# Taking the last eight tokens out of the expert-output matmuls of a 320-token sweep and adding them on VectorE

## What is computed

```
a = jax.nn.gelu(jnp.einsum('ted,td->te', u[ib], xb), approximate=False)
return jnp.einsum('te,ted->td', gb * a, v[ib])
```

## Time and profile before

| | |
|---|---|
| median of 3 runs | 4030.26 us (4028.16 to 4032.87) |
| the profiled execution's own time | 4045.91 us |
| its span | 4043.8 us |
| TensorE busy | 3878.7 us, 96% |
| table v, first to last matmul | 3099.6 to 4013.5 us |

### The profile page before, as it was taken

One profiled execution on the slowest core, in us unless ns is written; L12 is line 12 of the kernel. 1 busy time (PEld: TensorE's weight loads), 2 busy tenths in 40 slices (PEclk: granted clock), 3 DMA queues, 4 the chain that ended last, 5 costly groups with the idle time before them and its releaser, 6 DMA issues. The chain is left out here.

```text
span 4043.8 us, 70070 instructions
## 1 busy us (share of the span) xinstructions
PE 3878.7 (96%) x26200; PEld 3702.3 (92%) x26200; DVE 3054.3 (76%) x4083; ACT 1422.9 (35%) x2046; POOL 1570.5 (39%) x1349
## 2 busy tenths in 40 slices
PE   7999999999999887999999999999998999999997
PEld 7989988999999665989899999999997999999997
DVE  6875167777777433878589999999976888888887
ACT  5884122222223222223333333333333333333332
POOL 0000022233233112234116566666776455555551
PEclk9999999999999898999799999999998999999998
DMA  7988888999999796889579899888999999999996
GB/s 272 341 307 298 290 292 327 355 375 364 370 372 367 285 380 261 297 323 356 211 267 326 321 331 325 318 313 299 340 347 315 360 348 346 342 345 346 342 345 240
DMA packets 336051, 1310.12 MB, mean 324 GB/s; under 512 B 48912, under 2 KB 105392, under 8 KB 266304
## 3 DMA queue, kind: packets, MB, share of 16 engines
q1 hardware_dynamic: 201680, 646.09, 43.7%
q0 software_dynamic: 108848, 629.71, 42.2%
q10 hardware_dynamic: 25344, 31.99, 2.1%
HBM read 1237.86 MB, written 69.77 MB: 323 GB/s over the span
## 5 line engine op out<-in xcount | busy, mean ns | idle before, releaser
L2365 POOL DMA_INDIRECT routes_scratch<-gate_sums,route x384 | 463.8, 1208 | 165.8 <-issue 104.2
L130 PE MATMUL acc<-x_hi,w_hi 128*128 128x448 f32 x1296 | 476.9, 368 | 11.2 <-DVE w_lo L119 6.5
L130 PE MATMUL acc<-x_lo,w_hi 128*128 128x448 f32 x1296 | 474.9, 366 | 0.0
L130 PE MATMUL acc<-x_hi,w_lo 128*128 128x448 f32 x1296 | 474.8, 366 | 0.0
L114 ACT ACTIVATE w_hi<-w_raw 128x1024 fp32r<-128x1024 f32 x242 | 256.3, 1061 | 605.2 <-DMA w_raw<-in_w_gate 263.0
L119 DVE TENSOR_TENSOR w_lo<-w_raw,w_hi 128x1024 fp32r<-128x1024 f32 x242 | 295.3, 1222 | 178.7 <-ACT w_hi L114 178.0
L2777 POOL TENSOR_TENSOR tile_full<-act_and_gate 128x320 f32<-128x320 f32 x120 | 310.2, 2585 | 261.2 <-DVE tile_lo L2882 173.6
L2154 ACT ACTIVATE w_hi_a<-w_raw 128x1024 fp32r<-128x1024 f32 x270 | 279.3, 1057 | 287.4 <-PE acc L2954 250.2
L2172 PE MATMUL acc<-h_hi,w_hi_b 128*128 128x320 f32 (+1 forms) x1152 | 367.3, 319 | 13.3 <-DVE w_lo_b L2162 13.3
L2172 PE MATMUL acc<-h_hi,w_hi_a 128*128 128x320 f32 (+1 forms) x1152 | 370.4, 322 | 9.0 <-DVE w_lo_a L2162 7.7
L2172 PE MATMUL acc<-h_lo,w_hi_a 128*128 128x320 f32 (+1 forms) x1152 | 367.0, 319 | 0.0
(11 more groups left out here) (519 smaller groups left out, 10430.9 us busy)
## 6 DMA issues: line engine op xcount, KB each, us to landing
w_raw<-in_w_peer_u SPq DMA_DIRECT2D x256, 512.0 KB, 5.4
w_raw<-in_w_peer_v SPq DMA_DIRECT2D x256, 512.0 KB, 5.7
w_first<-in_w_gate SPq DMA_DIRECT2D x96, 512.0 KB, 4.9
w_raw<-in_w_gate SPq DMA_DIRECT2D x96, 512.0 KB, 7.1
w_first<-in_w_z SPq DMA_DIRECT2D x66, 512.0 KB, 5.2
w_raw<-in_w_z SPq DMA_DIRECT2D x66, 512.0 KB, 7.7
k_ring<-in_cache_k SPq DMA_DIRECT2D x64, 512.0 KB, 7.6
v_ring<-in_cache_v POOLq DMA_DIRECT2D x64, 512.0 KB, 8.6
```

The lines of the kernel that those rows point to most:

```text
L130: last = nc.tensor.matmul(dst, l_, r_[:, cc, 0:cn], start=(cc == first and p_ == 0), stop=(cc == last_c and p_ == 2))
L2365: pool.indirect_dma_start(route_dram, bass.IndirectOffsetOnAxis(ap=route[0:ROWS[b], b, n:n + 1], axis=0), gsum[0:ROWS[b], h % SUMS, b - 1, ...
```

## The change

Only 312 columns are left in the matmuls, tiles and sums of table v; the activations, routes and `out_t` are cut to them. Tokens 312 to 319 are computed as 8 tokens x 128 experts = 8 gathers of 128 rows: partition 16 t + j of gather k holds the row of rank 8 j + k of token t. SyncE sends the experts, routes and gates of the eight tokens through DRAM to turn them onto 128 partitions. GpSimd fetches the activations with eight indirect DMAs of one float for each partition, multiplies them by the gates, and issues the gathers, the first after step 3, then one in each place marked in the code. VectorE adds each gathered buffer, times its weight, into `sum8` (`last_row`), four matmuls with a 0/1 matrix add the 16 partitions of each token, and VectorE adds that to `x1`. There is one buffer for these rows.

```diff
+            def last_gather(k):
+                nc.gpsimd.tensor_copy(stage_8[:, 0:1], e8[...k...]).then_inc(s_8sg, 1)
+                pool.wait_ge(s_8sg, k + 1)
+                pool.sem_inc(s_8tick, 1)
+                pool.indirect_dma_start(row8[:], None, a["peer_v"], bass.IndirectOffsetOnAxis(ap=stage_8[:, 0:1], axis=0)).then_inc(s_8gat, 16)
...
-            with pool.Fori(1, (NTILE - GRP) // 2) as i:
+            rows(1, True)
+            pool.wait_ge(s_8ld, 48)
+            for k in range(VTOK):
+                pool.indirect_dma_start(a8[:, k:k + 1], None, acts_dram.rearrange("n p (t o) -> (n p t) o", o=1), bass.IndirectOffsetOnAxis(ap=r8[:, k:k + 1], axis=0)).then_inc(s_8a, 16)
+            pool.wait_ge(s_8a, 16 * VTOK)
+            nc.gpsimd.tensor_tensor(w8[:], a8[:], g8[:], ALU.mult).then_inc(s_8w, 1)
+            last_gather(0)
+            with pool.Fori(2, GRP) as i:
+                rows(i, True)
+            with pool.Fori(1, NG // 2 - 1) as gg:
+                pool.wait_ge(s_8used, gg + 1)
+                last_gather(gg)
+                with pool.Fori(0, GRP) as j:
+                    rows(GRP * gg + j, True)
+            pool.wait_ge(s_8used, VTOK)
+            last_gather(VTOK - 1)
+            with pool.Fori(GRP * (NG // 2 - 1), (NTILE - GRP) // 2) as i:
                 rows(i, True)
...
+            def last_row(k):
+                dve.wait_ge(s_8w, 1)
+                dve.wait_ge(s_8gat, 16 * k)
+                dve.wait_ge(s_8used, k)
+                nc.vector.scalar_tensor_tensor(out=sum8[:], in0=row8[:], scalar=w, in1=sum8[:], op0=ALU.mult, op1=ALU.add).then_inc(s_8used, 1)
...
+                nc.vector.memset(sum8[:], 0.0)
+                nc.vector.memset(pick[:], 0.0).then_inc(s_8used, 1)
...
             with eng.Fori(1 if start else 0, NG // 2 - 1) as gg:
+                each_group(gg)
                 for par in range(2):
...
+                if n == 0:
+                    last_row(VTOK - 1)
+                if n == 1:
+                    last_row(VTOK)
+                if n == 2:
+                    dve.wait_ge(s_8sum, 1)
+                    nc.vector.tensor_tensor(x3, tps[0:ROWS[3]].rearrange("p a c -> p (a c)"), x3, ALU.add)
...
-                        last = nc.tensor.matmul(acc[:, s, h, 0:ND], l_, r_[:, t_, :], start=(c == 0 and p_ == 0),
+                        last = nc.tensor.matmul(acc[:, s, h, 0:NV], l_, r_[:, t_, :], start=(c == 0 and p_ == 0),
...
+                if j == 2:
+                    for g in range(4):
+                        last = nc.tensor.matmul(tps[0:ROWS[3], g, :], pick[:], sum8[:, 512 * g:512 * (g + 1)], start=True, stop=True)
```

More of the change, by code:

```diff
@@ L2705, in build @@
         s_g3, s_b3 = sem("final_g_loaded"), sem("x1_block3_reloaded")
+        VTOK = 8
+        NV = ND - VTOK
         NG = NTILE // GRP
-        t_hi = at("tile_hi", [P, 2 * GRP, ND], F32R, O_R1)
-        t_lo = at("tile_lo", [P, 2 * GRP, ND], F32R, O_R1 + 2 * GRP * ND * 4)
+        NR = P // VTOK
+        t_hi = at("tile_hi", [P, 2 * GRP, NV], F32R, O_R1)
+        t_lo = at("tile_lo", [P, 2 * GRP, NV], F32R, O_R1 + 2 * GRP * ND * 4)
         ring_v = at("ring_v", [P, 2, D], F32, O_R1 + 4 * GRP * ND * 4)
-        out_t = at("out_t", [P, KC, ND], F32, O_T)
+        out_t = at("out_t", [P, KC, NV], F32, O_T)
         O_AG = O_T + KC * ND * 4
-        ag = at("act_and_gate", [P, 2, 2, ND], F32, O_AG)
-        hf = at("tile_full", [P, 2, ND], F32, O_AG + 4 * ND * 4)
+        ag = at("act_and_gate", [P, 2, 2, NV], F32, O_AG)
+        hf = at("tile_full", [P, 2, NV], F32, O_AG + 4 * ND * 4)
         stage_e = at("expert_stage", [P, 2, 8], I32, O_AG + 6 * ND * 4)
         assert O_AG + 6 * ND * 4 + 64 <= O_EARLY
+        row8 = at("rows_of_last_tokens", [P, D], F32, O_R1 + 4 * GRP * ND * 4 + 2 * D * 4)
+        sum8 = at("sum_of_last_tokens", [P, D], F32, O_R1 + 4 * GRP * ND * 4 + 3 * D * 4)
+        place = [O_T + KC * NV * 4]
+        e8, r8 = (then(x, [P, VTOK], I32) for x in ("last_experts", "last_routes"))
+        g8, a8, w8 = (then(x, [P, VTOK], F32) for x in ("last_gates", "last_acts", "last_weights"))
+        pick = then("last_token_of_row", [P, ROWS[3]], F32)
+        stage_8 = then("last_expert_stage", [P, 8], I32)
+        assert place[0] <= O_AG
+        s_8st, s_8ld, s_8a, s_8w, s_8sg, s_8tick, s_8gat, s_8used, s_8pick, s_8sum = (sem(f"last_tokens_{x}") for x in (
+            "stored", "loaded", "acts", "weights", "staged", "tick", "gathered", "used", "pick", "summed"))
         s_xback = sem("x1_last_reloaded")
@@ L2757, in table_v_sync @@
             load_tile(GRP + 1, 1)
+            last8 = slice(ROWS[3] - VTOK, ROWS[3])
+            for k, x_ in enumerate((eidx, route, gate.bitcast(I32))):
+                sp.dma_start(last8_dram[k], x_[last8, 3, :]).then_inc(s_8st, 16)
+            sp.wait_ge(s_8st, 48)
+            for k, x_ in enumerate((e8, r8, g8.bitcast(I32))):
+                sp.dma_start(x_[:], last8_dram[k].rearrange("t (j k) -> (t j) k", k=VTOK)).then_inc(s_8ld, 16)
             with sp.Fori(1, (NTILE - GRP) // 2) as i:
@@ L2798, in table_v_gpsimd @@
                 nc.gpsimd.memset(out_t[:, 4 * k:4 * k + 4, :], 0.0).then_inc(s_clr, 1)
+            def last_gather(k):
+                nc.gpsimd.tensor_copy(stage_8[:, 0:1], e8[:, k:k + 1] if isinstance(k, int) else e8[:, bass.ds(k, 1)]).then_inc(s_8sg, 1)
+                pool.wait_ge(s_8sg, k + 1)
+                pool.sem_inc(s_8tick, 1)
+                pool.indirect_dma_start(row8[:], None, a["peer_v"], bass.IndirectOffsetOnAxis(ap=stage_8[:, 0:1], axis=0)).then_inc(s_8gat, 16)
             def rows(i, build):
@@ L2812, in table_v_gpsimd, with sweep @@
                 rows(i, False)
-        def sweep(eng, before, split, after, beside, start=None):
+        def sweep(eng, before, split, after, beside, start, each_group):
             def body(first, par, j, build=True, ahead=True, between=None):
@@ L2875, in beside @@
                     nc.scalar.activation(ms2[:, 4:5], ms2[:, 4:5], ACT.Sqrt).then_inc(s_t0, 1)
-            sweep(act, before, lambda i, s: split_hi(act, i, s, q7), lambda *_: None, beside, lambda: None)
+            sweep(act, before, lambda i, s: split_hi(act, i, s, q7), lambda *_: None, beside, lambda: None, lambda gg: None)
         def table_v_vector(dve):
@@ L2931, in beside @@
                                                    op0=ALU.mult, op1=ALU.mult).then_inc(s_y0, 1)
-            sweep(dve, lambda *_: None, lambda i, s: split_lo(dve, i, s, q7), after, beside, sums_cleared)
+            sweep(dve, lambda *_: None, lambda i, s: split_lo(dve, i, s, q7), after, beside, sums_cleared, last_row)
         def table_v_tensor(pe):
@@ L2966, in table_v_tensor @@
                     half(0, 1, j, s, h)
-            with pe.Fori(1, NG // 2) as gg:
+            with pe.Fori(1, NG // 2 - 1) as gg:
                 for par in range(2):
@@ L2971, in table_v_tensor @@
                             half(gg, par, j, s, h)
+            with pe.Fori(0, GRP // 2) as j:
+                for s, h in QUARTERS:
+                    half(NG // 2 - 1, 0, j, s, h)
+            for j in range(GRP // 2):
+                if j == 2:
+                    pe.wait_ge(s_8used, VTOK + 1)
+                    pe.wait_ge(s_8pick, 1)
+                    pe.wait_ge(s_q0, 1)
+                    for g in range(4):
+                        last = nc.tensor.matmul(tps[0:ROWS[3], g, :], pick[:], sum8[:, 512 * g:512 * (g + 1)], start=True, stop=True)
+                    last.then_inc(s_8sum, 1)
+                for s, h in QUARTERS:
+                    half(NG // 2 - 1, 1, j, s, h)
         with nc.Block() as block:
@@ L3002, in build @@
         g_fin = g_row
+        NEW = [0, P, P, ROWS[3] - VTOK]
         y = at("y", [P, 2, D], F32, O_R1)
@@ L3031, in _ @@
                         for c in range(4):
-                            last = nc.tensor.transpose(tps[0:ROWS[b], g, c * P:(c + 1) * P],
-                                                       out_t[:, 4 * g + c, COLS[b]:COLS[b] + ROWS[b]], ident[:])
+                            last = nc.tensor.transpose(tps[0:NEW[b], g, c * P:(c + 1) * P],
+                                                       out_t[:, 4 * g + c, COLS[b]:COLS[b] + NEW[b]], ident[:])
                         last.then_inc(s_ft, 1)
@@ L3048, in add @@
                 def add(b):
-                    r = ROWS[b]
+                    r = NEW[b]
                     dve.wait_ge({1: s_back[0], 2: s_back[1], 3: s_b3}[b], 16)
```

18 lines of the change are left out of this document (12 added, 6 removed).

## The result

| | before | after |
|---|---|---|
| median | 4029.31 us (4028.16 to 4032.87, 4 runs) | 4075.33 us (4057.53 to 4084.01, 4 runs) |
| ratio | | 1.0093, 95% interval 1.0068 to 1.0119 |
| the profiled execution's own time | 4045.91 us | 4057.53 us |
| table v, first to last matmul | 913.9 us | 949.7 us |

The kernel is slower, by some 0.9%. The two medians of four runs alone would give 1.0114, which lies inside the interval. The median lies 5 us above the range that was given; by the ratio the time is 4067 us, inside it. The forecast of 4046 had the sign and the place right and less than half of the size.

A forecast was written before the change was run, and what follows sets the result against it. TensorE, busy for 96% of the span, was taken to pace the stage. Columns -21.4, seven waits +26, start +9 and four matmuls +2 make +16 us, moving the median from 4030.3 to 4046 us; 8-in-10 range 4026 to 4070.

The forecast's parts named there:

- Columns, -21.4 us: Table v's 6144 matmuls: each loses 8 columns, 3.49 ns a matmul, saving 21.4 us.
- The wait at seven places: Starts of passes 1 to 7: GpSimd waits for VectorE's `last_row`, making TensorE 3.7 us late each, 26 us in all.
- the second stall: Pass starts, half 132 in the replay of pass 4: late row gather makes TensorE 3.7 us late, first stall included.
- a first stall of 1.8 us: Pass starts, half 130 in the replay of pass 4: TensorE wants weights at 3570.0, VectorE has them at 3571.8.
- Mine of 1.8 stand between.: Stalls of 1.8 us lie between earlier idle times of 1.9 (clock dip followed) and 1.5 us (none); a dip costs 1.7.
- The landing of the gather: Row gather at a pass start lands 6.0 us after issue, the median of the earlier rows.
- The start, 9 us: First pass: GpSimd's eight small indirect DMAs delay halves 10 and 12; a stall of 7 us, 9 us in all.
- Covered work: Eighth `last_row` and 64-row addition in the last pass, SyncE's small DMAs at the start: nothing; uncovered 3 and 4 us.
- the hidden wait: Rival: the lead of ScalarE, VectorE and the halves swallows the pass-start waits; 4011 to 4020 us; chance 0.12.
- the quick landing: Rival: gathers land in 5.4 to 4.8 us, a pass start costs 3.1 to 2.5; 4034 to 4041 us; chance 0.16.
- the clock case: Rival: TensorE's stalls are followed by 1.2 GHz stretches, seven dips costing 12 us; 4056 to 4075 us; chance 0.15.
- DMA as the bound: Rival: added traffic finds no room, gain void and each of 8 gathers costs 3 us; 4065 us; chance 0.07.

The follow-up runs named there:

- narrow_only: Changed kernel with everything added for the last eight tokens taken out, leaving the 312 columns; ratio to the kernel before 0.9950.
- late_gather: Changed kernel with the wait and the last tokens' gather behind the first four steps of each pass; ratio to the kernel before 1.0000.
- wait_early_gather_late: Changed kernel with GpSimd's wait still at each pass start but the last tokens' gather issued four steps later; ratio to the kernel before 1.0081.
- changed_again: The changed kernel as it is, run again for a second profile; ratio to the kernel before 1.0102.
- late_and_spread: late_gather with the start's eight small DMAs in pairs behind steps 5, 7, 9, 11 and first gather behind step 13; ratio to before 0.9994.
- row_half_pass_early: Changed kernel with VectorE taking each last tokens' row eight steps earlier, GpSimd's queue unchanged; ratio to the kernel before 1.0023.
- all_moved: late_and_spread with VectorE's last tokens' row mid-pass and GpSimd's wait and gather behind the twelfth step; ratio to the kernel before 0.9979.

## Why the prediction was right or wrong, point by point

- **Columns, -21.4 us: right.** 21 us by the passes of narrow_only, 20 by its ratio. The pace of 320 and 448 columns gave the slope; the clock alone (20.5) would have done too.
- **The wait at seven places: right mechanism, wrong size.** That moving the wait takes the stalls away (late_gather), and that the wait without its gather keeps them (wait_early_gather_late), shows the cause. The term was 7 x 3.7 = 26 us, set by the second stall, that of the late row gather. Measured over 110.0 us (the last pass without the four matmuls) it is 5.2 + 6.1 + 6.1 + 6.1 + 5.6 + 6.2 + 6.0 = 41 us. Two steps of the replay were short, and the clock came on top:
  - *"VectorE's rest of half 130 ... is there at 3571.8", a first stall of 1.8 us.* TensorE wanted it at 3557.89 + 6.86 = 3564.75 and went on at 3568.34, 3.6 us late. The chain came about 0.6 us later than reckoned, and then the pair of rests took 3.43 us where it takes 2.35 otherwise, while GpSimd ran the product of tile 73 (3566.35) and a copy. The first of the two rests took 2.3 us at all fourteen pass starts of the two profiles of the changed kernel, the second 1.2. In the prediction GpSimd was held up by VectorE; I did not ask for the other direction. The Trainium skill, "SBUF — State Buffer", section "Who interferes with whom", says that a VectorE instruction with two SBUF inputs contends with a GpSimd instruction that reads SBUF, since its second input comes through the read interface that the two share. The rows agree that they hold each other up: VectorE lost 1.08 us against a product of 0.85. The Trainium skill adds there that the order of issue decides who is blocked. By the starts in the profile that does not come out here: VectorE's rest started 0.36 us ahead of the product and was the one that took longer. The kernel before had shown the same once, in its first pass, in VectorE's pair and GpSimd's product:

```profile
3130.16 3.30 DVE L2162 TENSOR_TENSOR w_lo_b<-w_raw,w_hi_b 128x1024 fp32r<-128x1024 f32 x2
```

```profile
3130.35 0.88 POOL L2777 TENSOR_TENSOR tile_full<-act_and_gate 128x320 f32<-128x320 f32 x1
```

  - *"it lands 6.0 us after ... 3576.0", a second stall that makes it 3.7 us in all.* In pass 4 of changed_again, without a dip, the row gather was issued 7.4 us after TensorE's first matmul of the pass (replay: 6.9), and VectorE's row started at 14.0 (replay: 12.9). Half 132 was then 4.7 us late. The 1.0 us over 3.7 comes with the row: 0.5 in the chain ahead of its issue and 0.6 in its landing, with 0.1 won behind it. The longer first stall does not add to this, as it ends before.
  - *"Mine of 1.8 stand between."* The first stall was 3.4 us idle, and in the first profile a clock dip shows behind six of the seven, in the second behind five. Four shorter stalls in wait_early_gather_late, 1.6 to 1.7 us idle, had none. With a dip a pass start costs 3.6 us for the first stall and up to 2.7 for the dip: 6.1 to 6.2 where the dip is long, and the second stall is hidden in it. So the longer first stall counts in these passes, and a dip, priced at 1.7 us, adds up to 1.4 (116.2 against 114.8). Without any dip the term would be 6 x 4.8 and 4.2 (pass 7 of changed_again, up to its middle), 33 us: of the 15 us that were missing some 7 are the late row, and the other 8 are the dips and the small gaps of pass 5 (115.6, without a dip).
- **The landing of the gather: about right.** Row 64 was issued at 3565.32 and used at 3571.98, 6.7 us against 6.0, with the queues empty before it. Over the stage the median rose from 6.0 to 8.1, though. It rose as much in late_gather (8.6), which has no such stalls, and not in narrow_only (6.0), so it goes with the added work and not with the stalls.
- **The start, 9 us: low.** The first pass lost 134.6 - (125.6 - 2.6) = 11.6 us in the first profile. But first passes scatter (narrow_only, without any of the new work, has 129.1), so no more can be said than that the stall at half 10 was there, 5.7 and 8.7 us in the two profiles of the changed kernel against the 7 of the replay, and went away in late_and_spread.
- **Four matmuls, 2 us: low.** They take 3.7. The trace has eight records for the four, of 592 ns each: the single time of the earlier trace rows was that of half a matmul. The same instructions, by line:

```profile
L3044 PE MATMUL tps<-sum_of_last_tokens,last_token_of_row x8: 592/592/643, 3994.4 to 3997.5; 128*64 128x512 f32 x8
```

- **Covered work: right but for one row.** `last_row` at step 120, the addition of 64 rows and SyncE's small DMAs show no gap of TensorE in the first profile. In changed_again there is one of 1.6 us at half 242, right behind `last_row` at step 120, where VectorE had waited 2.55 us for a row's gather just before: the picture of half 146 in row_half_pass_early. The idle time that was to cover it is not always there.
- **The sum.** The columns, the seven waits, the start and the four matmuls make, in the first profile: -20.9 + 41.3 + 11.6 + 3.7 = +35.7 us, the 35.8 of the stage. Of the rivals, the hidden wait and the quick landing are out; the clock case (4056 to 4075) was nearest, though the dips and the small gaps of pass 5 are only 8 of the 20 us that the sum was short of. DMA as the bound is out as the main cause: late_gather and all_moved carry the same bytes at 110.0 us a pass in four of six passes.

## What to carry to other kernels

A wait put into an in-order queue is priced by what stands behind it in that queue, and behind the waiter's waiters: here a 2 us gather for eight tokens held a product, a rounding, two weight parts and a row gather, at the one place where the chain has no lead. The same wait, four steps later, costs next to nothing; so put such work where what it waits for has long happened. When replaying a chain on VectorE and GpSimd, ask how each holds up the other, in both directions, and add what a stall does to the clock.

## What the runs showed of the hardware that was not expected

- A VectorE subtraction of 128x1024 from SBUF, 1.2 us, took some 1.1 us longer when GpSimd's product of 0.85 us ran beside it, although VectorE's had started 0.36 us earlier.
- The median time of a row gather from issue to landing rose from 6.0 us (before, narrow_only) to 8.6 (late_gather), though only one gather was added to the 16 of a pass.
- The clock: of ten stalls of 3.40 us idle in the two profiles of the changed kernel eight were followed by time at 1.2 GHz, and two by none: pass 5 of the first, and pass 4 of changed_again (1.00 from 3570.5 to 3586.0).
- A float32 matmul of 512 columns stands in the trace as two records of 0.59 us, and the four took 3.7 us, 0.9 each.
